# Softmax division inside the turning of the probabilities, and GpSimd adding two of three terms in the last stage

## The reference

```python
    sink_l = jnp.broadcast_to(..., s_loc.shape[:-1] + (1,))
    probs = jax.nn.softmax(jnp.concatenate([s_loc, s_ctx, sink_l], axis=-1), axis=-1)
    o = (jnp.einsum('bnkgij,bnjkd->bnikgd', probs[..., :n_loc].astype(v.dtype), vw)
         + jnp.einsum('bnkgic,bckd->bnikgd', probs[..., n_loc:n_loc + n_ctx].astype(vc.dtype), vc))
...
        x = layer_norm(RES_ALPHA * x + g2 * f, ln2_g[layer], ln2_b[layer])
```

## Time and profile before

| | us |
|---|---|
| median of three runs | 2583.0 (2582.92, 2583.0, 2587.47) |
| the profiled execution | 2587.05 |
| its span, first to last instruction | 2585.2 |
| TensorE busy | 2343.2 |
| VectorE busy | 939.2 |
| GpSimd busy | 464.7 |
| ScalarE busy | 407.0 |

### The profile page before, as it was taken

One profiled execution on the slowest core, in us unless ns is written; L12 is line 12 of the kernel. 1 busy time (PEld: TensorE's weight loads), 2 busy tenths in 40 slices (PEclk: granted clock), 3 DMA queues, 4 the chain that ended last, 5 costly groups with the idle time before them and its releaser, 6 DMA issues. The chain is left out here.

```text
span 2585.2 us, 39013 instructions
## 1 busy us (share of the span) xinstructions
PE 2343.2 (91%) x15084; PEld 1632.6 (63%) x15084; DVE 939.2 (36%) x2319; ACT 407.0 (16%) x1057; POOL 464.7 (18%) x608
## 2 busy tenths in 40 slices
PE   7999879997499999999949997899499999999997
PEld 5999745654466666666629985555266666666652
DVE  1777745665410110110126565465611111111114
ACT  1011133331011111111111113233000000000000
POOL 0000113444011111111111111344111111111111
PEclk9999979998699999999979998999699999999998
DMA  9655430001679999999832103100299999999955
GB/s 364 197 169 160 149 115 17 17 25 50 241 297 393 389 399 384 388 393 399 346 130 105 45 22 138 40 18 24 93 374 398 383 384 389 390 386 387 383 226 212
DMA packets 130991, 608.69 MB, mean 235 GB/s; under 512 B 20840, under 2 KB 23912, under 8 KB 112208
## 3 DMA queue, kind: packets, MB, share of 16 engines
q1 hardware_dynamic: 113456, 569.60, 57.0%
q0 software_dynamic: 16864, 37.78, 3.9%
q10 hardware_dynamic: 576, 0.02, 0.0%
HBM read 599.39 MB, written 42.02 MB: 248 GB/s over the span
## 5 line engine op out<-in xcount | busy, mean ns | idle before, releaser
L2062 PEld LDWEIGHTS gate_up<-room,w_gate_up 128*128 128x128 f32 x4608 | 522.5, 194 | 31.6 <-issue 31.6
L2062 PE MATMUL gate_up<-room,w_gate_up 128*128 128x128 f32 x4608 | 529.4, 277 | 3.2 <-DVE room L1942 3.2
L2071 PE MATMUL down<-w_down,room 128*128 128x512 f32 x576 | 256.8, 599 | 0.0
L2079 PE MATMUL gate_up_short<-w_gate_up,room 128*64 128x512 f32 x1152 | 255.1, 595 | 0.0
L1951 DVE TENSOR_TENSOR room<-room,gate_up 128x128 f32<-128x128 f32 x144 | 41.4, 288 | 540.4 <-ACT room L1982 540.4
L2079 PEld LDWEIGHTS gate_up_short<-w_gate_up,room 128*64 128x64 f32 x1152 | 79.4, 137 | 171.3 <-issue 171.3
L2071 PEld LDWEIGHTS down<-w_down,room 128*128 128x128 f32 x576 | 106.5, 190 | 123.0 <-issue 120.5
L1673 POOL COPY rows_idx<-slot_token 128x1 int32 (+1 forms) x78 | 14.4, 184 | 767.3 <-PE rows_turned L2049 710.7
L1959 DVE TENSOR_TENSOR room<-room,gate_up_short 128x256 f32<-128x256 f32 x36 | 15.2, 422 | 369.1 <-ACT room L1989 369.1
L2092 PE MATMUL down<-w_down,room 128*64 128x512 f32 x576 | 131.5, 598 | 11.9 <-ACT room L1991 11.9
L1453 PE MATMUL proj<-w_out,mixT 128*128 128x512 f32 x288 | 129.5, 592 | 0.0
(11 more groups left out here) (378 smaller groups left out, 3194.5 us busy)
## 6 DMA issues: line engine op xcount, KB each, us to landing
w_gate_up<-in_w_exp_gate SPq DMA_DIRECT2D x72, 2048.0 KB, 8.7
w_gate_up<-in_w_exp_up SPq DMA_DIRECT2D x72, 2048.0 KB, 13.3
w_down<-in_w_exp_down SPq DMA_DIRECT2D x72, 2048.0 KB, 12.2
ada_w<-in_w_ada SPq DMA_DIRECT2D x96, 512.0 KB, 4.6
h_rows<-h SPq DMA_DIRECT2D x18, 512.0 KB, 2.6
w_out<-in_w_out SPq DMA_DIRECT2D x2, 4096.0 KB, 13.5
w_in<-in_w_in SPq DMA_DIRECT2D x2, 3072.0 KB, 20.7
xn<-expert_rows SPq DMA_DIRECT2D x10, 512.0 KB, 3.9
```

Source lines behind the costliest of these rows:

```text
L2062: mm = nc.tensor.matmul(H[j % 2][:, o, :], wgu[0][:, o, k, j * P:(j + 1) * P], xT[0][:, k, :], start=k == 0, stop=k == KT - 1)
L2071: mm = nc.tensor.matmul(Y[:, h, :], hid[:, j, :], wd[0][:, j, h * 512:(h + 1) * 512], start=j == 0, stop=j == JT - 1)
L2079: mm = nc.tensor.matmul(Hs[c * HP:(c + 1) * HP, :, :], xT[1][:, k, :], wgu[1][:, :, k, c * 2 * P:(c + 1) * 2 * P], start=k == 0, stop=k == ...
```

## The change

In `attend` the division moves ahead of the turning. Turning a block was a product with the identity matrix (`nc.tensor.transpose`); now it is a real product (`nc.tensor.matmul`) of the block with a diagonal matrix of the reciprocals, so that the turned block comes out divided. VectorE makes the diagonals itself, with operations that take one tensor and one or two scalars per partition, once for each pair; `turn_probs` waits for them (`diag_ready`) instead of for the exponentials (`expd`). GpSimd's `diagonals`, TensorE's `spread_den` and VectorE's `heads` are gone, and ScalarE copies the heads' output straight to `mixT`. In `finish`, for tiles 2 to 7, ScalarE scales `x` and `yb`, GpSimd adds them, and TensorE adds the sum with a single product by the identity; tiles 0 and 1 stay as they were.

```diff
-                def diagonals(t):
-                    pool.wait_ge(den_ready, t + 1)
-                    if t:
-                        pool.wait_ge(rb_full, t)
-                    nc.gpsimd.tensor_tensor(dg[:, :, :], across(g.k[:, K_ID:K_ID + P], NH), over(den[:, :], P), ALU.mult).then_inc(diag_ready, 1)
...
-                def denominators(t):
-                    v.wait_ge(expd, t * 2 + 2)
-                    if t:
-                        v.wait_ge(diag_ready, t)
-                    small(nc.vector.tensor_tensor(den[:, :], sums[:, 1, :], se[:, :], ALU.add))
+                def denominators(t, pair):
+                    v.wait_ge(expd, t * 2 + pair + 1)
+                    for h in (pair, pair + 2):
+                        small(nc.vector.tensor_scalar(den[:, h:h + 1], sums[:, 1, h:h + 1], se[:, h:h + 1], sums[:, 0, h:h + 1], ALU.add, ALU.add))
                     done()
-                    small(nc.vector.tensor_tensor(den[:, :], den[:, :], sums[:, 0, :], ALU.add))
+                    small(nc.vector.reciprocal(den[:, pair:NH:2], den[:, pair:NH:2]))
                     done()
-                    nc.vector.reciprocal(den[:, :], den[:, :]).then_inc(den_ready, 1)
-
-                def heads(t):
-                    v.wait_ge(rb_read, t + 1)
-                    nc.vector.tensor_tensor(ys[t % 2][:, 0:2, :], O[:, 0:2, :], rb[:, :, :], ALU.mult).then_inc(o_ready, 1)
+                    for i, h in enumerate((pair, pair + 2)):
+                        d = nc.vector.tensor_scalar(dg[:, pair, i, :], g.k[:, K_ID:K_ID + P], den[:, h:h + 1], None, ALU.mult)
+                    d.then_inc(diag_ready, 1)
...
                     if rtr(t):
                         norm2(t - 2)
+                    if t and att(t):
+                        denominators(t, 0)
                     if prj(t):
                         residual(t - 1, 0)
                     if att(t):
                         maxima(t, 1)
                         if t == 0:
+                            denominators(0, 0)
+                            denominators(0, 1)
                             v.wait_ge(small_in, 80)
                         gate_out(t)
-                        denominators(t)
+                        if t:
+                            denominators(t, 1)
...
-                        nc.scalar.activation(rb[:, :, :], O[:, 2:4, :], ACT.Copy).then_inc(rb_read, 1)
+                        nc.scalar.activation(ys[t % 2][:, 0:2, :], O[:, 0:2, :], ACT.Copy).then_inc(o_ready, 1)
...
                 def turn_probs(t, pair):
-                    pe.wait_ge(expd, t * 2 + pair + 1)
+                    pe.wait_ge(diag_ready, t * 2 + pair + 1)
                     flat = pr[pair][:, :, :].rearrange("p a n -> p (a n)")
                     for j, group in enumerate(blocks(t)):
-                        turn(("probs", t, pair, j), [flat[:, b * P:(b + 1) * P] for b in group])
+                        b, n = turn_of["probs", t, pair, j]
+                        if n:
+                            pe.wait_ge(T_read[b], n)
+                        for i, k in enumerate(group):
+                            mm = nc.tensor.matmul(T[b][:, i, :], flat[:, k * P:(k + 1) * P], dg[:, pair, k // 5, :], start=True, stop=True)
+                        mm.then_inc(T_full[b], 1)
...
                     if att(t):
-                        spread_den(t)
                         values(t, 1)
...
             @block.gpsimd
             def _(pool):
+                def add_x(t):
+                    pool.wait_ge(scaled, t - 1)
+                    nc.gpsimd.tensor_tensor(yb[:, t, :], yb[:, t, :], g.x[:, t, :], ALU.add).then_inc(added, 1)
+
+                add_x(2)
                 for t in range(LT):
+                    if t and t + 2 < LT:
+                        add_x(t + 2)
                     pool.wait_ge(var_ready, t + 1)
...
+                for t in range(2, LT):
+                    nc.scalar.activation(g.x[:, t, :], g.x[:, t, :], ACT.Copy, scale=ALPHA)
+                    act.wait_ge(landed[t], 32)
+                    nc.scalar.activation(yb[:, t, :], yb[:, t, :], ACT.Copy, scale=g.gate[:, t, 1:2]).then_inc(scaled, 1)
...
+                    else:
+                        pe.wait_ge(landed[t], 32)
+                        for h in range(2):
+                            nc.tensor.matmul(S[t % NS][:, h, :], diag[:, t, 0, :], ya[:, t, halves[h]], start=True, stop=False)
+                        pe.wait_ge(added, t - 1)
+                        for h in range(2):
+                            mm = nc.tensor.matmul(S[t % NS][:, h, :], g.k[:, K_ID:K_ID + P], yb[:, t, halves[h]], start=False, stop=True)
```

More of the change, by code:

```diff
@@ L1319, in exps @@
                         act.wait_ge(T_full[b], n + 1)
-                        if pair == 0:
-                            act.wait_ge(den_ready, t)
                     near, far = near_of(t, pair), far_of(t, pair)
@@ L1433, in gate @@
                     mm.then_inc(gate_full, 1)
-                def spread_den(t):
-                    pe.wait_ge(diag_ready, t + 1)
-                    for pair in range(2):
-                        for kv in range(NKV):
-                            mm = nc.tensor.matmul(O[kv * HD:(kv + 1) * HD, 2 + pair, :], g.k[:, K_ONE:K_ONE + HD], dg[:, 2 * kv + pair, :], start=True, stop=True)
-                    mm.then_inc(rb_full, 1)
                 def project_half(u, half):
@@ L2113, in finish @@
         NS = 3
+        whole = lambda t: t < 2
         S = [psum(f"sum{i}", [P, 2, 512]) for i in range(NS)]
@@ L2146, in _ @@
                 for t in range(LT):
-                    for k in range(2):
+                    for k in range(2 if whole(t) else 1):
                         d = nc.scalar.activation(diag[:, t, k, :], g.k[:, K_ID:K_ID + P], ACT.Copy, scale=g.gate[:, t, k:k + 1])
                     d.then_inc(diag_ready, 1)
+                for t in range(2, LT):
+                    nc.scalar.activation(g.x[:, t, :], g.x[:, t, :], ACT.Copy, scale=ALPHA)
+                    act.wait_ge(landed[t], 32)
+                    nc.scalar.activation(yb[:, t, :], yb[:, t, :], ACT.Copy, scale=g.gate[:, t, 1:2]).then_inc(scaled, 1)
             @block.vector
@@ L2190, in _ @@
                         pe.wait_ge(centred, t - NS + 1)
-                    for h in range(2):
-                        nc.tensor.matmul(S[t % NS][:, h, :], alpha[:, :], g.x[:, t, h * 512:(h + 1) * 512], start=True, stop=False)
-                    pe.wait_ge(landed[t], 32)
-                    for h in range(2):
-                        for k, y in enumerate((ya, yb)):
-                            mm = nc.tensor.matmul(S[t % NS][:, h, :], diag[:, t, k, :], y[:, t, h * 512:(h + 1) * 512], start=False, stop=k == 1)
+                    halves = [slice(h * 512, (h + 1) * 512) for h in range(2)]
+                    if whole(t):
+                        for h in range(2):
+                            nc.tensor.matmul(S[t % NS][:, h, :], alpha[:, :], g.x[:, t, halves[h]], start=True, stop=False)
+                        pe.wait_ge(landed[t], 32)
+                        for h in range(2):
+                            for k, y in enumerate((ya, yb)):
+                                mm = nc.tensor.matmul(S[t % NS][:, h, :], diag[:, t, k, :], y[:, t, halves[h]], start=False, stop=k == 1)
+                    else:
+                        pe.wait_ge(landed[t], 32)
+                        for h in range(2):
+                            nc.tensor.matmul(S[t % NS][:, h, :], diag[:, t, 0, :], ya[:, t, halves[h]], start=True, stop=False)
+                        pe.wait_ge(added, t - 1)
+                        for h in range(2):
+                            mm = nc.tensor.matmul(S[t % NS][:, h, :], g.k[:, K_ID:K_ID + P], yb[:, t, halves[h]], start=False, stop=True)
                     mm.then_inc(summed, 1)
```

17 lines of the change are left out of this document (6 added, 11 removed).

## The result

The changed kernel takes 2601.9 us (median of four runs, 2600.79 to 2605.14) where the kernel before took 2583.9 beside it (four runs, 2582.92 to 2587.47). The ratio is 1.0074, with a 95% interval from 1.0061 to 1.0087: 0.7% slower, where I had forecast 0.4% faster, and outside the range of 2562 to 2598. The profiled execution of the changed kernel took 2600.79 us with a span of 2599.0.

What follows compares the result with a forecast made beforehand. The prediction took TensorE, busy for 91% of the span, as the bound, except for waits in the first `attend` tiles. Terms of -19 + 8 + 4 - 4 = -11 us gave 2572 us, own range 2566 to 2580, 8-in-10 range 2562 to 2598.

Steps and rivals of the forecast that it cites:

- What bounds the kernel: In `attend`, TensorE hardly waits in later tiles, but in each stage's first tile it waits 8.00 and 7.03 us.
- Term 1: First tile of each `attend` stage: TensorE no longer waits for GpSimd, about 19 us less.
- Term 2: Later `attend` tiles: real products for turning, less L1439 removed, cost 0.5 us a tile, about 8 us more.
- Term 3: Later `attend` tiles: VectorE's diagonals come 0.3 us late in 12 tiles, about 4 us more.
- operand count: Later `attend` tiles: diagonal products, having one SBUF tensor, go on beside GpSimd's 2.36 us multiplication of `h`.
- rival A: Later `attend` tiles: diagonal products wait for GpSimd's multiplication, TensorE starts 1.9 us late; +9 us, 2592; chance 0.20.
- Term 4: Last stage: fewer TensorE instructions in tiles 2 to 7, against GpSimd's new addition; about 4 us less.
- B: Later `attend` tiles: second diagonal product also waits for GpSimd's next operation, TensorE 4.2 us late; +38, 2621; chance 0.12.

Runs made afterwards that it cites:

- The move ahead of `h`: Changed kernel with VectorE's sums, reciprocal and diagonal products of pair 0 put ahead of the second norm's last operation: 2576.7 us, ratio 0.998.
- the accumulating form: Changed kernel with VectorE's diagonal products also writing their row sum into a scratch column that nothing reads: 2583.6 us, ratio 1.0005.
- undivided turning: Changed kernel with blocks turned by the identity as before, diagonals still made and waited for, division left out: 2661.4 us, ratio 1.0317.
- the kernel with `add_one` moved: Kernel before the change with GpSimd's add_one(0) moved behind the diagonals of tile 0, nothing else changed: 2561.7 us, ratio 0.9917.

## Why the prediction was wrong

**What bounds the kernel: right.** The two regimes of `attend` showed as told, waits in the first tile and a busy TensorE in the others.

**Term 1 (-19): measured -16.** 8.4 and 7.6 us. Turning began 8.8 us after the stage's first scores, 0.2 later than taken. The clock rose at 364 to 366, 6 us after it and not 4, so that the 40 instructions took 7.8 us instead of 6.6.

**Term 2 (+8): right in kind, mis-sized, some +20.** I had +0.58 for pair 0 and +0.32 for pair 1, less the 0.49 of L1439. Pair 0 from 436.94 to the scores at 439.49 is 2.55 where it was 1.72, +0.83, and pair 1 from 450.00 to the turned `h` at 452.83 is 2.83 where it was 1.98, +0.85. From the turned `h` to the values it is 1.00 where it was 1.48, and to the next scores 3.11 where it was 3.55 (before, 455.47, 456.95 and 459.02; now 452.83, 453.83 and 455.94): 0.44 of the 0.49 came back. That is 1.24 a tile, two and a half times the 0.5 that I took, and above my bound, which I gave as 1.1 though its parts make 0.9. The fault was to go by 20 x 0.115 = 2.3 us for turning: to the next work it is 2.55 and 2.83. Over 16 tiles 1.24 is 20 us.

**Term 3 (+4): this step failed.** "I follow the operand count, with the opposite as a rival." The operand count was the wrong rule. The product has one SBUF tensor, but in the form that runs at double rate it waits for GpSimd's 2.34 us operation as one with two tensors does: 2.10 against 2.17 us for two. Turning begins 1.87 us later in 12 tiles, 22.4 us in all, the 1.9 of rival A, whose order (neither product waited for GpSimd's next operation, L1142) showed as well. The earlier trace rows had the double rate in plain sight, and the earlier trace rows were of another form. The move ahead of `h`, 25 us faster, shows that GpSimd's operation is what the products wait for, and the accumulating form, slower by itself and 18 us faster in the kernel, that the form of the product decides whether they do.

The Trainium skill (SBUF — State Buffer, Who interferes with whom) states this rule, and excepts the form of `tensor_scalar` that also writes out its accumulator. Both halves agree with the runs here: 2.10 us for two products without the accumulator, a maximum of 0.347 for one with it.

**Term 4 (-4): near in number, in part by luck.** The stage is 5.0 us shorter, but the tiles themselves only 2.3: they fell into step at 4.07 us instead of the 4.4 that I took, and the start cost more than the 1.4 that I took (0.8 in the first tile, 2.6 in the second, where L2172 paid 3.30). The other 2.7 us lie ahead of the first statistics, which come 9.0 us after the stage's beginning and came 11.8 after it before. That is not the change's: the kernel with the old last stage and the new `attend` has 9.4 there, the one with the new last stage and the old `attend` 11.8.

**The sum.** -16 + 20 + 22.4 - 5 = +21.4, against +19.4 by the stages and +18.0 by the medians. Layer 1 has 7 x 1.24 + 6 x 1.87 - 7.6 = +12.3 against +13.8; behind its first wait, of 1.93 us, the clock of the changed kernel fell, and that tile took 1.5 us more than the same one of layer 0, whose clock did not fall:

```profile
1662.00:1664.00 2.00, 2.00 (x12) 2.00 (x10) 1.96 (x3) 1.05 (x2) 0.89 (x1) 0.50 0.13 53
```

Layer 0 has 9 x 1.24 + 6 x 1.87 - 8.4 = +14.0 against +10.6. Here the clock gives the difference. In the profiled execution of the kernel before it fell within 588 to 598 us, in the context tiles; in the kernel with the old `attend` and the new last stage, which has the same work there, it did not. The rows of the two:

```profile
588.00:598.00 10.00, 9.82 (x36) 5.41 (x37) 4.17 (x14) 2.34 (x12) 6.83 (x6) 0.66 0.01 2
```

```profile
588.00:598.00 10.00, 10.00 (x47) 5.49 (x44) 5.41 (x14) 2.94 (x13) 6.83 (x6) 1.00 0.01 2
```

With its 288.9 us for layer 0 (351.95 to 640.89) in place of 292.7, the changed `attend` costs +14.4, as its terms say. The fall comes and goes with old and new `attend` alike: the kernel with the changed `attend` and the old last stage had it, too, and took 304.5.

**The rivals.** Rival A was 2592, made of its wait and my small term 2; with term 2 as measured it would have been 2604. The chance that I gave to A and B together, 0.32, was low for a question that I had marked as open and for which one of the two kinds of evidence, the rate, pointed to them.

## What to carry to other kernels

A VectorE operation that ran at double rate waited for GpSimd here as one with two tensors did, although it has one: before such an operation is put into a critical chain, look what GpSimd does at that moment, and put it ahead of GpSimd's long operation, or take a form without the double rate. Turning by a real f32 product is not a free division: it cost 1.1 to 1.4 us a tile where TensorE is the bound. And when a change frees a wait in one tile only, ask first what else would free it: moving one line of GpSimd's program gave 20 us, more than the 16 that the first tiles gained here, and added no work.

## What the runs showed of the hardware

**The clock behind a wait.** In the kernel with undivided turning TensorE's clock fell behind six of the twelve waits for the diagonals (in layer 0, from 434 us on, in every second tile), and a tile of layer 0 took 29.8 us with the fall and 28.29 without. The rows of the windows behind the waits at 434.7 and 464.5 us (PEclk is the third number from the end):

```profile
438.00:440.00 2.00, 2.00 (x15) 1.56 (x12) 0.87 (x3) 0.00 (x0) 0.00 (x0) 0.50 0.54 215
...
466.00:470.00 4.00, 4.00 (x26) 2.69 (x27) 3.87 (x7) 0.74 (x2) 0.69 (x1) 1.00 0.34 135
```

The changed kernel has the same waits, with real products in place of transpositions behind them. Behind its twelve waits the clock fell once, at 1662 us, as shown above. So the real products may have given back part of the 1.4 us that they cost: with transpositions behind the wait the clock fell more often. The Trainium skill (TensorE: Matmul & The Clock Gate, Part 4: PE-mode transpose) says that transpositions don't count as work for the clock as matmuls do. This pair of traces fits, though the undivided kernel also has shorter stretches of work; in the trace of the next paragraph the clock rose, though the work ahead of the step was transpositions and only at its end 1.12 us of products.

**The place of the clock's step is partly chance.** In the kernel with `add_one` moved, whose first tile turns by transpositions (357.41 to 363.86 with a pause of 1.44, then the gate's products), the clock rose in this window, as in the changed kernel:

```profile
364.00:366.00 2.00, 0.91 (x8) 0.51 (x6) 0.93 (x3) 0.28 (x1) 0.00 (x0) 0.71 1.00 401
```

In the kernel before, with the same work up to that point, the values at 368.18 took 2.40 us for 20 instructions, against 1.31 here. In layer 1 of the kernel with `add_one` moved the same values take 2.40 us again. In layer 0 of both, `attend` had begun at full clock, which fell within 354 to 356 us, but the stage itself began at 350.4 us here and at 352.5 in the kernel before. So the same work can meet the step or miss it, and that is worth 1 to 2 us in a first tile: 10.2 us were gained in layer 0 (350.38 to 369.25, against 29.1 before) and 8.1 in layer 1 (1581.50 to 1601.69, against 28.3). With the new last stage added it was the other way round: 20.1 us to the next scores in layer 0, 18.9 in layer 1. That the place of the start decides it is argued, not shown.
